# Two stages of an expert layer put into one: gates finished head by head, products paced by TensorE

## The reference

```python
q = (xt @ wq).reshape(-1, PEER_HEADS, 2, PEER_HALF)
s = jnp.einsum('thpc,hpnc->thpn', q, keys)
sv, si = lax.top_k(s, PEER_TOPK)                  # 16 of 128, for each half
cand = sv[:, :, 0, :, None] + sv[:, :, 1, None, :]
cid = si[:, :, 0, :, None] * N_KEYS + si[:, :, 1, None, :]
top_s, top_j = lax.top_k(cand, PEER_TOPK)         # 16 of 256
eid = jnp.take_along_axis(cid, top_j, axis=-1)
gate = jax.nn.softmax(top_s.astype(jnp.float32), axis=-1)
act = jax.nn.gelu(jnp.einsum('thkd,td->thk', ue, xt), approximate=False)
return jnp.einsum('thk,thkd->td', (gate * act), ve)
```

## Time and profile before

| | us |
|---|---|
| runs, median of 3 | 3188.28 (3187.27 to 3194.87) |
| the profiled execution's own time | 3186.14 |
| its span | 3184.5 |
| PE busy | 2920.6 (92%) |
| DVE busy | 1782.8 (56%) |
| ACT busy | 1423.2 (45%) |
| POOL busy | 626.3 (20%) |

### The profile page before, as it was taken

How to read it: one execution, slowest core, us unless ns; L and a number is a source line. 1 busy time by engine, 2 the same in 40 slices (tenths; PEclk the granted TensorE clock), 3 DMA queues, 4 the chain that set the end, 5 groups by cost and what they waited for, 6 DMA issues and landing times. The chain is left out here.

```text
span 3184.5 us, 54921 instructions
## 1 busy us (share of the span) xinstructions
PE 2920.6 (92%) x17320; PEld 2551.2 (80%) x17320; DVE 1782.8 (56%) x3239; ACT 1423.2 (45%) x2600; POOL 626.3 (20%) x488
## 2 busy tenths in 40 slices
PE   6879997799989699987798999999998999999996
PEld 4658784688757599966698999999998778888885
DVE  5784325532355665446687874444445985555556
ACT  6663234422444344443344444444444445555553
POOL 0030001200000000010000028778775750000000
PEclk9999998799989799988899999999999999999998
DMA  6873237332425355534454567877777876666664
GB/s 237 288 229 127 87 111 278 93 122 96 139 85 180 99 182 188 165 126 134 162 167 154 181 185 181 182 184 180 183 184 243 278 237 193 193 192 192 194 193 132
DMA packets 182878, 554.10 MB, mean 174 GB/s; under 512 B 53664, under 2 KB 53696, under 8 KB 179488
## 3 DMA queue, kind: packets, MB, share of 16 engines
q1 hardware_dynamic: 137696, 517.03, 50.1%
q0 software_dynamic: 44544, 32.10, 6.2%
q10 hardware_dynamic: 576, 4.19, 0.3%
HBM read 532.13 MB, written 21.10 MB: 174 GB/s over the span
## 5 line engine op out<-in xcount | busy, mean ns | idle before, releaser
L153 DVE TENSOR_TENSOR w_lo<-raw,w_hi 128x512 fp32r<-128x512 f32 x1888 | 1319.0, 724 | 1175.8 <-ACT w_hi L146 1173.0
L146 ACT ACTIVATE w_hi<-raw 128x512 fp32r<-128x512 f32 x1888 | 1144.4, 629 | 989.9 <-PE PS L164 924.7
L162 PE MATMUL PS<-h_hi,w_hi 128*128 128x256 f32 x2944 | 833.9, 283 | 14.1 <-ACT L1753 8.6
L163 PE MATMUL PS<-h_lo,w_hi 128*128 128x256 f32 x2944 | 831.2, 282 | 0.0
L164 PE MATMUL PS<-h_hi,w_lo 128*128 128x256 f32 x2944 | 831.1, 282 | 0.0
L162 PEld LDWEIGHTS PS<-h_hi,w_hi 128*128 128x128 f32 x2944 | 564.7, 192 | 16.6 <-issue 10.9
L164 PEld LDWEIGHTS PS<-h_hi,w_lo 128*128 128x128 f32 x2944 | 564.8, 192 | 0.0
L163 PEld LDWEIGHTS PS<-h_lo,w_hi 128*128 128x128 f32 x2944 | 564.7, 192 | 0.0
L1725 POOL DMA_INDIRECT g_dram<-gt,spot x256 | 418.2, 1634 | 528.0 <-DVE gt L1853 417.9
L162 PE MATMUL PS<-w_hi,wj_hi 128*128 128x512 f32 x1024 | 402.8, 393 | 20.4 <-DVE wj_lo L1925 20.1
L164 PE MATMUL PS<-w_hi,wj_lo 128*128 128x512 f32 x1024 | 400.2, 391 | 0.0
(11 more groups left out here) (315 smaller groups left out, 2909.8 us busy)
## 6 DMA issues: line engine op xcount, KB each, us to landing
raw<-in_u_s SPq DMA_DIRECT2D x256, 512.0 KB
raw<-in_v SPq DMA_DIRECT2D x256, 512.0 KB
raw<-in_w_in_s SPq DMA_DIRECT2D x112, 512.0 KB
raw<-in_w_mod_s SPq DMA_DIRECT2D x96, 512.0 KB
raw<-in_w_in_a SPq DMA_DIRECT2D x64, 512.0 KB
raw<-in_w_in_b SPq DMA_DIRECT2D x64, 512.0 KB
raw<-in_w_out_s SPq DMA_DIRECT2D x64, 512.0 KB
g_dram<-h_buf SPq DMA_DIRECT2D x1, 16384.0 KB, 42.7
```

The costliest lines, as they stand in the source:

```text
L146: act.activation(w_hi[m % 2][:, half], raw[:, m % NRAW, half], ACT.Copy).then_inc(hi_ready, 1)
L153: dve.tensor_tensor(w_lo[m % 2][:, half], raw[:, m % NRAW, half], w_hi[m % 2][:, half].bitcast(F), ALU.subtract).then_inc(lo_ready, 1)
L162: pe.matmul(out, lhs[0], rhs[0], start=start, stop=False)
L163: pe.matmul(out, lhs[0], rhs[1], start=False, stop=False)
```

## The change

The two stages become one block. DVE finishes the gates of a head (`finish`) while it searches the next one; the largest score of the same head is subtracted, inside `picks`. ACT takes one exponential a head (`gate_exp`). POOL waits for each head apart before it scatters it. The multiply of gates into `wt` waits until PE has come within eight experts (`weigh`), for the first ones already during the end of the scoring. Scoring accumulates in banks 6 and 7, and the first weighted slab uses banks 0, 1, 4 and 5. `wj_hi` and `wj_lo` lie where `si`, `spot` and `gt` were.

```diff
+            wj_at = nc.sbuf_base
             si = buf3("si", [P, TT, 2 * HEADS, TOPK], F, ph)
+            spot = buf3("spot", [P, TT, HEADS, TOPK], U32, ph)
             gt = buf3("gt", [P, TT, HEADS, TOPK], F, ph)
+
+            wj_hi, wj_lo = ([nc.alloc_sbuf_tensor_at(f"{x}{i}", [P, T], R, offset=wj_at + (2 * n + i) * T * 4) for i in range(2)]
+                            for n, x in enumerate(("wj_hi", "wj_lo")))
...
+                    load_slabs(sp, src_v, base["v"], NRAW, N_V)
...
-                    pool.wait_ge(g_ready, 1)
...
+                        pool.wait_ge(g_ready, h + 1)
...
+                    def weigh(reg, n):
+
+                        b = n // 2 % GB
+                        pool.wait_ge(acc_free, past(reg, n + 4))
+                        wait_multiplied(pool, None if reg is None else reg * 2, v0 + 2 * n - 16)
+                        pool.wait_ge(g_in[b], past(reg, 16 * (n // (2 * GB) + 1), 2))
+                        two = wt[:, n:n + 2, :] if reg is None else wt[:, ds(reg + n, 2), :]
+                        pool.tensor_tensor(two, two, pick[:, b, :].rearrange("p (j t) -> p j t", j=2), ALU.mult)\
+                            .then_inc(weighed, 2)
+
+                    def fetch(reg, n):
+                        two = g_by_row[:, n:n + 2, :] if reg is None else g_by_row[:, ds(reg + n, 2), :]
+                        pool.dma_start(pick[:, n // 2 % GB, :].rearrange("p (j t) -> p j t", j=2), two)\
+                            .then_inc(g_in[n // 2 % GB], 16)
+
+                    for n in range(0, 2 * GB, 2):
+                        fetch(None, n)
+                    for n in range(0, 2 * GB, 2):
+                        weigh(None, n)
+                        pool.wait_ge(weighed, n + 2)
+                        fetch(None, n + 2 * GB)
+                    wait_multiplied(pool, None, v0)
+                    pool.wait_ge(h_stored, 16)
+                    pool.dma_start(hb[:, :, :], h_dram).then_inc(late_in, 16)
+                    for i, name in enumerate(("ln2_g", "ln2_b")):
+                        pool.dma_start(par[i][:, :], bcast(io[name])).then_inc(late_in, 16)
+                    with loop(pool, N_KEYS - 4 * GB, 2 * GB) as j:
+                        for n in range(2 * GB, 4 * GB, 2):
+                            weigh(j, n)
+                            pool.wait_ge(weighed, j + (n + 2))
+                            fetch(j, n + 2 * GB)
+                    for n in range(N_KEYS - 2 * GB, N_KEYS, 2):
+                        weigh(None, n)
...
+                            feature_slab(pe, PS[:, 6 + j % 2, 0:T], r2, m0 + 2 * j + half, half, h_hi, h_lo, slice(0, T))
...
+                    expert_slab(None, v0, 0, 0, True, False)
+
+                    pe.wait_ge(acc_free, N_KEYS + 2)
+                    expert_slab(None, v0 + 1, 0, 1, True, False)
...
+                    def experts(reg, j):
                         r2 = None if reg is None else reg * 2
+                        for s in range(2):
+                            round_slab(act, r2, m0 + 2 * j + s + 1)
                         wait_multiplied(act, r2, m0 + 2 * j + 2)
-                        act.activation(wt[:, j if reg is None else reg + j, :], PS[:, j % 2, 0:T], ACT.Gelu).then_inc(acc_free, 1)
+                        act.activation(wt[:, j if reg is None else reg + j, :], PS[:, 6 + j % 2, 0:T], ACT.Gelu).then_inc(acc_free, 1)
+
+                    def gate_exp(at, n):
+                        act.wait_ge(sh, n)
+                        act.activation(gt[:, :, at, :], gt[:, :, at, :], ACT.Exp).then_inc(g_exp, 1)
                     act.preload_act_table(ACT.Gelu)
                     act.sem_inc(acc_free, 2)
-                    with loop(act, J1, 2) as j:
+
+                    for j in range(4):
+                        experts(None, j)
+                    with loop(act, HEADS - 1) as h:
+                        for j in range(4, 8):
+                            experts(h * 4, j)
+                            if j == 5:
+                                gate_exp(ds(h, 1), h + 1)
+                    for j in range(J1, J1 + 2):
+                        experts(None, j)
+                    gate_exp(slice(HEADS - 1, HEADS), HEADS)
+                    with loop(act, N_KEYS - J1 - 2, 2) as j:
                         for u in range(2):
+                            experts(j, J1 + 2 + u)
...
-                        dve.tensor_copy(gt[:, :, h, :], t8[:, :, :])
...
+                        for t in range(TT):
+                            i = dve.tensor_scalar(gt[:, t, at, :].rearrange("p h k -> p (h k)"), t8[:, t, :], t8[:, t, 0:1], None,
+                                                  ALU.subtract)
+                        i.then_inc(sh, 1)
...
+                    def finish(reg, h):
+                        at = slice(h, h + 1) if reg is None else ds(reg + h, 1)
+
+                        def row(x, t):
+                            return x[:, t, at, :].rearrange("p h k -> p (h k)")
+                        dve.wait_ge(tk, past(reg, (h + 1) * per + 1, per))
+                        for t in range(TT):
+                            i = dve.scalar_tensor_tensor(row(eid[:, :, 0], t), row(eid[:, :, 0], t), float(N_KEYS), row(eid[:, :, 1], t),
+                                                         ALU.mult, ALU.add)
+                        i.then_inc(gk, 1)
+                        dve.wait_ge(g_exp, past(reg, h + 1))
+                        dve.tensor_reduce(gs[:, :, at, 0], gt[:, :, at, :], X, ALU.add).then_inc(gk, 1)
+                        dve.wait_ge(gk, past(reg, 3 * h + 1, 3))
+                        for t in range(TT):
+                            dve.tensor_scalar(row(spot, t), row(eid[:, :, 0], t), float(T), place[:, t:t + 1], ALU.mult, ALU.add)
+                        dve.wait_ge(gk, past(reg, 3 * h + 2, 3))
+                        dve.reciprocal(gs[:, :, at, 1], gs[:, :, at, 0]).then_inc(gk, 1)
+                        dve.wait_ge(gk, past(reg, 3 * h + 3, 3))
+                        for t in range(TT):
+                            i = dve.tensor_scalar(row(gt, t), row(gt, t), gs[:, t, at, 1], None, ALU.mult)
+                        i.then_inc(g_ready, 1)
...
-                    for t in range(TT):
-                        both_keys = eid[:, t, 0, :, :].rearrange("p h k -> p (h k)")
-                        step(dve.scalar_tensor_tensor(both_keys, both_keys, float(N_KEYS),
-                                                      eid[:, t, 1, :, :].rearrange("p h k -> p (h k)"), ALU.mult, ALU.add))
-                        dve.tensor_scalar(spot[:, t, :], both_keys, float(T), place[:, t:t + 1], ALU.mult, ALU.add)
-                    for t in range(TT):
-                        i = dve.tensor_tensor(gt[:, t, :, :], gt[:, t, :, :], gs[:, t, :, 0:1].broadcast_to([P, HEADS, TOPK]),
-                                              ALU.subtract)
-                    i.then_inc(sh, 1)
-                    for s in range(2):
-                        split_slab(dve, None, m0 + 2 * J1 + s + 1)
-                    dve.wait_ge(g_exp, 1)
-                    step(dve.tensor_reduce(gs[:, :, :, 0], gt[:, :, :, :], X, ALU.add))
-                    step(dve.reciprocal(gs[:, :, :, 1], gs[:, :, :, 0]))
-                    for t in range(TT):
-                        i = dve.tensor_tensor(gt[:, t, :, :], gt[:, t, :, :], gs[:, t, :, 1:2].broadcast_to([P, HEADS, TOPK]),
-                                              ALU.mult)
-                    i.then_inc(g_ready, 1)
-                    for s in range(2, 4):
-                        split_slab(dve, None, m0 + 2 * J1 + s + 1)
...
+                    dve.sem_inc(tk, 1)
+                    picks(None, 0)
+                    with loop(dve, HEADS - 1) as h:
+                        picks(h, 1)
+                        finish(h, 0)
+                    for s in range(4):
+                        split_slab(dve, None, m0 + HEADS * HEAD_SLABS + s + 1)
+                    finish(None, HEADS - 1)
+                    with loop(dve, N_U - HEADS * HEAD_SLABS - 4, NRAW) as i:
```

More of the change, by code:

```diff
@@ L1743, in _, with expert_slab @@
-                    with loop(pe, N_KEYS - J2, 2) as j:
-                        for u in range(2):
-                            experts(j, J2 + u)
+                    def expert_slab(j, m, n, a, first, last_one):
+                        if a == 0:
+                            pe.wait_ge(wj_split, past(j, n + 1))
+                        for c in range(2):
+                            pe.wait_ge(lo_ready, halves(None if j is None else j * 2, m) + (c + 1))
+                            col = slice(c * 512, (c + 1) * 512)
+                            for t in range(TT):
+                                tok = slice(t * P, (t + 1) * P)
+                                last = mm3(pe, PS[:, 4 * t + 2 * a + c, :], (wj_hi[n % 2][:, tok], wj_lo[n % 2][:, tok]),
+                                           (w_hi[m % 2][:, col], w_lo[m % 2][:, col]), first, last_one)
```

(30 more changed lines are left out.)

170 lines of the change are left out of this document (41 added, 129 removed).

## The result

The changed kernel takes 3227.74 us (median of 4 runs, 3226.68 to 3230.02), the kernel before 3187.78 us beside it: ratio 1.0124, 95% interval 1.0112 to 1.0137. I had forecast 3165 us.

What follows compares the result with a forecast made beforehand. PE, busy 92% of the span, was taken as the bound. Terms -7.8 - 21.6 + 6.0 = -23.4 us took 3186.1 to 3162.7; with 2.1 for the median of runs, 3165 us, range 3156 to 3181.

Steps and rivals of the forecast that it cites:

- Part 1: Border between scoring and weighted sum: one block cuts PE's gap from 9.59 to 1.77 us, 7.8 us less.
- Part 2: Weighted sum: pacing POOL's gate multiplies removes the whole loss in the first 28 experts, 21.6 us less.
- Rival A: Weighted sum: POOL's multiply hits `wj_lo` and makes it late; 28 us, 3193 us; chance 0.06.
- rival B: Search: small DVE instructions are held by POOL's scatter issues; 70 us, over 3230 us; chance 0.03.
- Part 3: Search: ACT's table load for each head's exponential makes PE late by 0.75 us, eight times; 6.0 us more.
- Part 4: Search: DVE's added `finish`, 1.2 to 1.8 us a head, is covered by waits; cost 0, up to 1 us a head.
- Rival C: Search overflows: ACT's loads and `finish` together cost PE 2 us a head; +10 us, 3175 us; chance 0.13.

Runs made afterwards that it cites:

- e8_late_loads: Changed kernel with exponentials in ACT's idle time, plus `hb` and parameters loaded in four pieces behind the last four multiplies: 3155.90 us, ratio 0.9890.
- e3_paced_only: Kernel before, with only the pacing wait on the gate multiplies added; two blocks and one exponential kept: 3169.19 us, ratio 0.9943.
- e6_unpaced: Changed kernel with exponentials in ACT's idle time, without the wait that paces the multiplies: 3173.05 us, ratio 0.9952.
- e1_preload: Changed kernel plus one load of gelu's table right behind the eighth exponential, ahead of the scoring loop: 3172.71 us, ratio 0.9958.
- e2_exp_before_loop: Kernel before, its one exponential moved past two gelus to directly ahead of the scoring loop: 3242.30 us, ratio 1.0169.
- e10_finish_later: Changed kernel plus the one gelu table load ahead of the loop, with DVE's `finish` moved behind the search: 3174.03 us, ratio 0.9966.

## Why the prediction was wrong, step by step

**Part 1, the border: right.** The last scoring matmul starts at 2502.27, the first weighted one at 2504.23, so the gap is 1.84 us with the slot of 0.12 taken off; forecast 1.77. PE's clock stayed whole here, and that was in part luck. The prediction took no cost, since waits up to 1.3 us had left the clock at 0.98 and its rows showed none between that and the border's. The trace of before has one, just behind the 2600 us at which the earlier trace rows ends, and from 2604.4 to 2607.7 us, between two stretches of the earlier trace rows, the granted clock is 0.50:

```profile
2603.01 0.49 PE L162 MATMUL PS<-w_hi,wj_hi 128*128 128x512 f32 x1 [2.43 <-DVE wj_lo L1925]
```

In the changed kernel the 1.84 us of waiting ahead of 1910.50 are followed by half clock too, and so are 1.91 us at this very border in e8_late_loads. Scatter, first and last start:

```profile
L1740 POOL DMA_INDIRECT g_dram<-gt,spot x256: 1546/1550/3586, 1747.3 to 2281.3; - x128
```

Forecast 1742 to 2270, at a start of scoring 3 us earlier.

**Part 2, paced multiplies: right.** 697.73 us against 696.3. The load of `hb`, with 0 to 4 us as bounds and taken at 0 because no wait of before ends with a slab, does make ACT wait for one now, and PE starts the matmul at 2521.7 us 1.0 us late:

```profile
2519.29 1.15 ACT L146 ACTIVATE w_hi<-raw 128x512 fp32r<-128x512 f32 x2 [2.61 <-DMA raw<-in_v]
```

`wj_lo` is never long, and a multiply stretches one `w_lo` in two experts, as placed: 60 of the 510 in this stage take over 0.9 us, 10.9 us apart.

```profile
L1826 DVE TENSOR_TENSOR wj_lo<-wt,wj_hi x128: 418/419/425, 2503.8 to 3195.3; 128x256 fp32r<-128x256 f32 x128
```

The Trainium skill's page SBUF — State Buffer, "Who interferes with whom", says that a DVE instruction with two SBUF inputs and a GpSimd one that reads SBUF exclude each other; e3_paced_only and e6_unpaced agree (698 against 710 to 718 us). Rival A did not occur.

Of rival B only a trace is there. The timeline of DVE in the changed kernel, a first `finish` with no scatter beside it and one with the scatter running:

```profile
1745.51 0.37 DVE L1957 TENSOR_SCALAR spot<-eid,place  x2
...
1794.79 0.28 DVE L1950 SCALAR_TENSOR_TENSOR eid<-eid  x2
1795.20 0.61 DVE L1957 TENSOR_SCALAR spot<-eid,place  x2
...
1796.76 0.76 DVE L1902 TENSOR_TENSOR eq<-sv 128x256 f32 x2 [0.46 <-issue]
```

and that of POOL at the same time:

```profile
1794.10 2.23 POOL L1740 DMA_INDIRECT g_dram<-gt,spot  x1 [0.30 <-issue]
1796.64 1.55 POOL L1740 DMA_INDIRECT g_dram<-gt,spot  x1 [0.30 <-issue]
```

No DVE instruction is held for the length of an issue of 1.55 us; the longest in the search beside the scatter takes 0.75 us, a `w_lo`. The pair for `spot` takes 0.61 us instead of 0.37, the issue beside it 2.23 instead of 1.55, and `finish` in all 1796.76 - 1794.79 = 1.97 us.

**Part 3, the exponential per head: the step that failed.** It failed at three points; the time of a load itself was right.

*What was not in the sum at all: 52 us, the loop.* Of the missing 67.3 - 6.0 = 61.3 us the loop has 51.8, the last exponential 3.7 - 0.75 = 2.9, the search some 7. I counted table loads by the exponentials, 16 in all, and took the plain copy to need no table. I did not ask which table is active where a loop is entered. Before, two gelus stand between the exponential and the loop; after, the eighth exponential stands directly ahead of it, while the loop's body ends with gelu. The two ways into the body then bring different tables, and the program holds a load ahead of the body's first function, a copy, and one ahead of its first gelu, in each pass. That the differing ways are the reason is my reading, from where the loads stand and from two experiments; no view names the table that a load brings. e1_preload and e2_exp_before_loop show it from both sides: -52 us of scoring with the loads gone, +54 with the order alone. None of my rivals held it. The Trainium skill's page ScalarE activation tables: per-element evaluation and per-set limits, "Table sets in the compiler and the runtime", says that the back end places loads per block; I had not weighed it; the 47 and 47 loads of the loop's body agree with it.

*"The second load, for the next gelu, falls into the 2.35 us idle": wrong, 0.5 us a head.* In the unrolled code of before the load ran ahead of the wait: it started at 1884.68 us, while the gelu before, at 1879.53, puts PE's next release at about 1885.3. In the loop of the search it stands behind the wait, so it starts when PE is done and delays the next rounding:

```profile
1732.69 0.39 ACT L1836 ACTIVATE wt<-PS 128x256 f32 x1 [2.36 <-PE PS L164]
1733.10 1.28 ACT L1840 ACT_TABLE_LOAD   x1
1734.39 0.23 ACT L1840 ACTIVATE gt<-gt  x1
1734.53 2.17 ACT L146 ACTIVATE w_hi<-raw 128x512 fp32r<-128x512 f32 x4
1739.17 1.28 ACT L1836 ACT_TABLE_LOAD   x1 [2.47 <-PE PS L164]
1740.47 0.38 ACT L1836 ACTIVATE wt<-PS 128x256 f32 x1
...
1745.43 0.38 ACT L1836 ACTIVATE wt<-PS 128x256 f32 x1 [2.50 <-PE PS L164]
```

1732.69 to 1739.17 is 6.48 us, 0.72 over 5.76: the stall I had sized at 0.75. 1739.17 to 1745.43 is 6.26, the 0.50 of the late load.

*What follows a long wait: nothing in the sum, 1.5 us.* At the last exponential two loads stand ahead of the copy, one of them the loop's first. PE waits 2.0 us instead of 0.75, and then runs at half clock from 1911.0 to 1914.4 us, 1.5 us more.

*No drain, as the prediction held against the page.* By the Trainium skill's 1.38 us of drain (ScalarE: Activation LUTs, "What ACT_TABLE_LOAD costs") beside each load a pair of loads would cost more than shown: here the exponential starts 1.29 us behind its load's start, the load 0.03 us behind the end of the gelu.

**Part 4, DVE in the search: right alone, wrong beside part 3.** At just under 2 us `finish` is a little over the 1.2 to 1.8 estimated. I wrote that what the late `w_hi` shifts is caught up; with the second late load it is not, and DVE costs PE 0.55 us a head (e10_finish_later): 0.72 + 0.50 + 0.55 are the head's 1.8 us. Rival C had this mechanism and gave 2 us a head where 1.8 came; the search made 7 of the missing 61 us.

## What to carry to other kernels

Where a function of another table set comes near a loop, list the table loads with the loop's passes counted, and ask which set is active on both ways into the body: one load behind the last foreign function, or a function of the loop's own set between (two gelus in the kernel before), settles it. Put a foreign function where ACT would wait anyway, ahead of the wait, and ask for the old table at once. When a long burst on POOL slows DVE, move it to a stage where DVE has room or pace it; here pacing gave 20 us, more than twice what the border gave, and moving it gave 21 and took back 4.

## What was not expected of the hardware

A plain copy costs a table load of 1283 ns when the program puts one ahead of it; the copy itself takes 0.63 us behind such a load and, in e1_preload, without one, so the load bought nothing here. The clock stayed at 1.00 behind PE's 1.7 us of idle time at the border, where 9.4 us of idle time before had brought it to 0.76 on average; but waits only a little longer, 1.8 to 1.9 us, were followed by 3.4 us at half clock at eight places in five kernels, while others, up to 1.99 us in e2_exp_before_loop, were not. A slowed loop is only half seen in PE's waits, 28.3 us in 93 of them in the scoring loop, which lost 52; matmuls counted in a stretch show it better, 4484 in 591 us.
